# A two-block transformer kernel: loads, roundings and splits of its expert stages in another order, norm sums over two added tiles

## The reference, cut to what matters

```python
def rmsnorm(x, g):
    y = x * lax.rsqrt(jnp.mean(x * x, axis=-1, keepdims=True) + EPS)
    return y * g

def peer_ffn(h, w_q, sub_keys, u_tab, v_tab):      # h: normed, 512 x 1024
    q = (h @ w_q).reshape(B, L, 8, 2, 128)         # 8 heads, two halves
    s = einsum('blhpd,pnd->blhpn', q, sub_keys)    # 128 keys for each half
    top_s, top_i = lax.top_k(s, 16)
    ...                                            # the best 16 of the 16 x 16 sums, idx and gate
    act = gelu(einsum('bpd,bphkd->bphk', h, u_tab[idx]))
    return einsum('bphk,bphkd->bpd', act * gate, v_tab[idx])
```

## Time and profile before

| What | us |
|---|---|
| median of three runs | 2179.35 |
| the profiled execution | 2177.73 |
| its span | 2175.9 |
| TensorE busy (matmuls) | 2115.4 (97%) |
| VectorE busy | 1304.1 (60%) |
| GpSimd busy | 1033.5 (47%) |
| ScalarE busy | 922.6 (42%) |

### The profile page before, as it was taken

How to read it: one execution, slowest core, us unless ns; L and a number is a source line. 1 busy time by engine, 2 the same in 40 slices (tenths; PEclk the granted TensorE clock), 3 DMA queues, 4 the chain that set the end, 5 groups by cost and what they waited for, 6 DMA issues and landing times.

```text
span 2175.9 us, 27394 instructions
## 1 busy us (share of the span) xinstructions
PE 2115.4 (97%) x10296; PEld 1661.6 (76%) x10296; DVE 1304.1 (60%) x2244; ACT 922.6 (42%) x1528; POOL 1033.5 (47%) x892
## 2 busy tenths in 40 slices
PE   8999999999999999999999998999999899999999
PEld 6877767557887776887878877777778788888887
DVE  6456257352235774215898957888881666666664
ACT  4223343572234234111334447777773434343432
POOL 6655546212324122877859887999996100000000
PEclk9999999999999999999999999999999999999999
DMA  5222312201111111233216664777788988888884
GB/s 201 100 78 78 116 61 90 90 30 49 59 40 59 59 55 43 97 122 110 78 59 199 205 206 141 272 289 246 272 291 294 333 300 286 289 284 300 288 287 149
DMA packets 98291, 359.32 MB, mean 165 GB/s; under 512 B 8480, under 2 KB 41504, under 8 KB 73328
## 3 DMA queue, kind: packets, MB, share of 16 engines
q1 hardware_dynamic: 98160, 357.56, 47.3%
HBM read 286.09 MB, written 71.30 MB: 164 GB/s over the span
## 4 chain that ended last, share of the span: by engine, by line
PE 67%; POOL 13%; DVE 11%; issue 6%; ACT 2%; DMA 1%; POOLq 0%; SPq 0%; ACTq 0%; DVEq 0%
PE ps L1438 11%; PE ps L1439 11%; PE ps L802 10%; PE ps L803 9%; PE ps L804 9%; POOL area L2643 6%; POOL wring_parts L2621 6%; PE ps L791 2%; PE ps L1249 2%; DVE area L2413 2%; PE ps L1386 1%; PE ps L1387 1%; DVE area L2410 1%; PE ps L884 1%; PE ps L1225 1%
## 5 line engine op out<-in xcount | busy, mean ns | idle before, releaser
L2577 POOL CAST wring_parts<-wring 128x512 fp32r<-128x512 f32 x236 | 170.5, 764 | 546.0 <-PE ps L804 429.3
L1386 PE MATMUL ps<-sqbuf_parts,wring_parts 128*128 128x512 f32 x1024 | 412.6, 403 | 5.5 <-POOL wring_parts L2621 5.5
L1387 PE MATMUL ps<-normed_x_parts,wring_parts 128*128 128x512 f32 x1024 | 404.4, 395 | 0.0
L2621 POOL TENSOR_TENSOR wring_parts<-wring_parts,wring 128x512 fp32r<-128x512 f32 x256 | 331.0, 1323 | 76.0 <-ACT wring_parts L1856 73.0
L2581 POOL TENSOR_TENSOR wring_parts<-wring,wring_parts 128x512 fp32r<-128x512 f32 x244 | 351.2, 1470 | 6.6 <-ACT wring_parts L1852 1.5
L1386 PEld LDWEIGHTS ps<-sqbuf_parts,wring_parts 128*128 128x128 f32 x1024 | 194.0, 189 | 50.6 <-POOL wring_parts L2621 4.9
L1387 PEld LDWEIGHTS ps<-normed_x_parts,wring_parts 128*128 128x128 f32 x1024 | 193.9, 189 | 41.8
L802 PE MATMUL ps<-resid_parts,wring_parts 128*128 128x512 f32 (+1 forms) x528 | 201.2, 381 | 6.1 <-DVE normed_x_parts L2010 3.3
L803 PE MATMUL ps<-normed_x_parts,wring_parts 128*128 128x512 f32 (+1 forms) x528 | 197.0, 373 | 0.0
L804 PE MATMUL ps<-resid_parts,wring_parts 128*128 128x512 f32 (+1 forms) x528 | 196.2, 372 | 0.0
L1474 ACT ACTIVATE area<-ps 128x1024 f32<-128x1024 f32 (+6 forms) x89 | 61.7, 696 | 275.2 <-PE ps L804 183.5
(11 more groups left out here) (269 smaller groups left out, 4431.4 us busy)
## 6 DMA issues: line engine op xcount, KB each, us to landing
wring<-in_weights_dram SPq DMA_DIRECT2D x65, 1024.0 KB, 4.8
wring<-in_uT_dram SPq DMA_DIRECT2D x128, 512.0 KB, 4.4
area<-in_vT_dram SPq DMA_DIRECT2D x44, 1024.0 KB, 7.2
hidden_table<-area SPq DMA_DIRECT2D x32, 1024.0 KB, 6.7
gate_table<-area SPq DMA_DIRECT2D x32, 1024.0 KB, 8.4
area<-gate_table SPq DMA_DIRECT2D x32, 1024.0 KB, 9.1
wring<-in_vT_dram SPq DMA_DIRECT2D x20, 1024.0 KB, 6.7
rt<-hidden_table SPq DMA_DIRECT2D x32, 512.0 KB, 4.6
```

Source lines behind the costliest of these rows:

```text
L1386: pe.matmul(out, first[:, d], h_first[:, k, :], start=(k == 0), stop=False)
L1387: mm = pe.matmul(out, rest[:, d], h_rest[:, k, :], start=False, stop=(k == KD - 1))
L2577: ins = nc.gpsimd.tensor_copy(up[:, d, :], W(name)[:, d, :])
L2621: ins = nc.gpsimd.tensor_tensor(rest[:, a:a + PIECE], first[:, a:a + PIECE], u_raw[t % len(USLOT)][:, a:a + PIECE], ALU.subtract)
```

## The change

Five things are edited. The loads of the first two value halves are issued five tiles sooner, behind the wait for the stores of the stage's first half only. ScalarE rounds values 2 and 3 behind the first two coefficients, not among the last Gelus, and VectorE makes the rest of coefficients 1 ahead of that of values 2 and 3. ScalarE rounds tiles 0 and 1 at the start of its turn for head 6, and GpSimd splits them at the start of its turn for head 1, tiles 2 and 3 at the start of its turn for head 2. In the three norms VectorE adds the first three pairs into one tile (4), and TensorE sums tiles 4 and 6 alone. The copy of a quad into the stage runs over experts outside and tokens inside, where it ran the other way round; what is written is the same.

```diff
@@ -728,11 +730,12 @@
                 if t == EG * (BEFORE + BESIDE):
                     while parts:
                         store_piece(*parts.pop(0))
-                if t == TILES - len(USLOT) - 1:
+                if t == EG * (BEFORE + BESIDE) + 4:
 
                     sp.wait_ge(stored[0], 8 * PIECES * STORES)
                     load_v(0)
                     load_v(1)
+                if t == TILES - len(USLOT) - 1:
 
                     sp.wait_ge(stored[1], 8 * PIECES * STORES)
                     sp.wait_ge(spread, QUADS)
@@ -893,13 +896,15 @@
                 sq = norm_sq(name)[:, 0:KD * width].rearrange("p (k t) -> p k t", k=KD)
                 for m in pairs:
                     if name in ADDED:
-                        pe.wait_ge(pair_added, 4 * ADDED.index(name) + m + 1)
+                        if m >= 2:
+                            pe.wait_ge(pair_added, 2 * ADDED.index(name) + m - 1)
                     else:
                         pe.wait_ge(squares, 4 * BIG.index(name) + m + 1)
-                    for k in (2 * m,) if name in ADDED else (2 * m, 2 * m + 1):
+                    for k in ADDED_TILES[m] if name in ADDED else (2 * m, 2 * m + 1):
                         for at, n in ((0, T), (T, META)) if width == TM else ((0, T),):
                             mm = pe.matmul(flat(key)[:, at:at + n], ones, sq[:, k, at:at + n],
-                                           start=(k == 0), stop=(m == 3 and k == (6 if name in ADDED else 7)))
+                                           start=(k == ADDED_TILES[2][0] if name in ADDED else k == 0),
+                                           stop=(k == ADDED_TILES[3][0] if name in ADDED else k == KD - 1))
                 if pairs[-1] == 3:
                     fills(mm, key)
 
@@ -1857,12 +1862,12 @@
                                ).then_inc(u_rounded, 1)
 
             for h in range(HP):
+                if h == HP - 2:
+                    round_u(0)
+                    round_u(1)
                 if h + 1 < HP:
                     query(h + 1)
                 copy_out(("ps", h), sc[:, h].rearrange("p a b -> p (a b)"), flat(("ps", h)))
-                if h == HP - 2:
-                    round_u(0)
-                    round_u(1)
             round_u(2)
             round_u(3)
 
@@ -1927,12 +1932,13 @@
                 for j in range(EG):
                     gelu(g, j)
                     beside(EG * g + j)
-                    if g >= GROUPS - 2 and j % 2:
-                        if (g, j) == (GROUPS - 2, 1):
-                            act.wait_ge(stored[1], 8 * PIECES * STORES)
-                        round_v(2 * (g + 2 - GROUPS) + j // 2)
+                    if g == GROUPS - 2 and j % 2:
+                        round_v(j // 2)
             for n in range(2):
                 round_coefs(n)
+            act.wait_ge(stored[1], 8 * PIECES * STORES)
+            round_v(2)
+            round_v(3)
             round_coefs(2)
             round_coefs(3)
             for n in range(CSLOTS, HALVES):
@@ -1999,7 +2005,14 @@
 
                 sq = sqbuf[:, 0:KD * width].rearrange("p (k t) -> p k t", k=KD)
                 dve.wait_ge(squares, 4 * BIG.index(name) + m + 1)
-                dve.tensor_tensor(sq[:, 2 * m, :], sq[:, 2 * m, :], sq[:, 2 * m + 1, :], ALU.add).then_inc(pair_added, 1)
+                ins = dve.tensor_tensor(sq[:, 2 * m, :], sq[:, 2 * m, :], sq[:, 2 * m + 1, :], ALU.add)
+                if m in (1, 2):
+                    link(ins)
+                    ins = dve.tensor_tensor(sq[:, 2 * m, :], sq[:, 2 * m, :], sq[:, 2 * m - 2, :], ALU.add)
+                if m < 2:
+                    link(ins)
+                    return
+                ins.then_inc(pair_added, 1)
 
             def split_norm(turn, name, gain, width, between={}):
 
@@ -2499,9 +2512,9 @@
                 if i == 0 and piece >= 2:
 
                     dve.wait_ge(stored[piece % 2], 16 * STORES * (piece // 2))
-                dst = stage[:, piece % 2, :].rearrange("p (j t) -> p t j", t=HALF)
+                dst = stage[:, piece % 2, :].rearrange("p (j t) -> p j t", t=HALF)
                 dve.wait_ge(spread, n + 1)
-                dve.tensor_copy(dst[:, 4 * i:4 * i + 4, :], spread_out(n)).then_inc(copied, 1)
+                dve.tensor_copy(dst[:, :, 4 * i:4 * i + 4], spread_out(n).rearrange("p t n -> p n t")).then_inc(copied, 1)
 
             def split_v(n):
                 dve.wait_ge(v_rounded, n + 1)
@@ -2541,9 +2554,9 @@
             multiply_coefs(0)
             multiply_coefs(1)
             split_coefs(0)
+            split_coefs(1)
             split_v(2)
             split_v(3)
-            split_coefs(1)
             for n in range(2, HALVES):
                 multiply_coefs(n)
                 if n >= CSLOTS:
@@ -2624,8 +2637,8 @@
 
             split = 0
             for h in range(HP):
-                if h == 2:
-                    for split in range(4):
+                if h in (1, 2):
+                    for split in range(2 * h - 2, 2 * h):
                         split_u(split)
                 weigh_places(h)
                 if h < 2:
```

More of the change, by code:

```diff
@@ L302 @@
 ADDED = ["post", "mix", "ffn"]
+ADDED_TILES = ((), (), (4,), (6,))
 def build(nc, A):
```

## The result

The changed kernel takes 2186.06 us (median of 12 runs, 2183.57 to 2190.26) against 2178.05 us for the kernel before (12 runs, 2172.72 to 2183.91): a ratio of 1.004, 95% interval 1.0031 to 1.0049. It is 8.0 us slower; the forecast was 8.8 slower. The profiled execution took 2190.26 us, the slowest of the twelve, with a span of 2188.5, 12.6 above the span of the one before.

A forecast was written before the change was run, and what follows sets the result against it. TensorE, two thirds of the chain of waits, was taken as the bound. Terms 15.9 + 1.6 - 1.8 - 1.4 - 1.4 - 1.8 - 1.7 - 0.5 + 0.9 - 1 = +8.8 on the 2179.35 us median gave 2188, range 2173 to 2200.

The forecast's parts named there:

- The first tiles' split: GpSimd waits for tile 0 ahead of the last query's weights; less waiting and no low clock at tile 0: together +14.3 us.
- the three terms ahead of tile 0: Last query starts later, +15.9 us; low clock after that idleness, +1.6; shorter TensorE wait before tile 0, -1.8.
- The "-1.4": At tile 0, TensorE's shorter idleness of about 1.1 us brings no low clock: -1.4 us.
- Both sides move by the same amount, and that slack stays: End of routing: VectorE runs some 14.5 us later, its 11.9 us wait for turned entries stays; no cost.
- Handover: Second expert stage: no ScalarE wait for the first value tile, -1.4 us; a value rounding moved behind the coefficients, -1.8.
- Norms: Fewer sum matmuls on TensorE: post -1.7 us, ffn -0.5, mix +0.9 from a longer idle stretch with low clock.
- Copy: VectorE's copy into the stage lies between 701 and 1089 ns, shortening only the spreading stage's start: -1 us.
- (b): Strided PSUM read exceeds VectorE's spare time; above 1.5 us a copy, each further 0.1 costs 13 us; chance 0.12.
- (a): GpSimd before the last query: tile 0 is rounded early, no hold-up; sum -8.7 us, 2170.6; chance 0.08.
- (c): Spreading stage: a faster copy returns TensorE's idleness there and at its start, down to 2173 us; chance 0.09.
- (d): Tile loads behind the value loads leave TensorE without a tile: +4 us, 2192; chance 0.04.

## Why the prediction was right

The sign, the cause and the size held. Step by step, with the second pair of profiles beside the first (its spans differ by +8.9 us, those of the first by +12.6):

- **The first tiles' split, +14.3.** The gap ahead of the last query grew by 15.84 us (forecast 15.9), by the order of work that the step gives: the tile's rounding, two tiles, places, weights. All of it lies 2.7 us earlier than written (the copy ahead of the rounding at 1115.82 for 1118.55, the first split at 1117.86 for 1120.6, the last query at 1132.71 for 1135.5). Half of that is chance: when the kernel before was profiled again, it was 1.4 us earlier at the same place. Counted from the last sum of the ffn norm, tile 0 starts behind 104.06 us in both profiles of before and behind 119.79 and 119.86 in those of after: +15.7 and +15.8, where the three terms ahead of tile 0 (15.9 + 1.6 - 1.8) give 15.7. After the gap the last query's first matmul took 0.77 us (0.47 before), the low clock of the step; and tile 0 waited 1.31 us in place of 2.94, at the full clock. The "-1.4" held too: tile 1 starts 3.79 us behind tile 0 in both profiles of after, 5.23 and 5.35 in those of before. In the second profile of before the first four matmuls of tile 0 still ran at the full clock (0.47 us for the first), and the clock fell behind them, as its window shows:

```profile
1135.70:1138.70 3.00, 2.77 (x9) 2.24 (x10) 2.97 (x19) 2.54 (x3) 3.00 (x4) 0.72 0.00 0
```

- **"Both sides move by the same amount, and that slack stays": no term.** The slack did stay: VectorE waits 12.0 us for the turned entries, 11.9 before. What the step had no term for is TensorE's waits for later splits, which VectorE's long additions bring about: 4.9 us in the profile of after, 1.4 in that of before. By the terms the stretch behind tile 0 was to shrink by 1.4 us (the low clock). It grew by 3.6 in the first pair, and shrank by 1.5 in the profiles taken again (176.0 against 177.5), where the waits are 2.9 and 3.2 us. So the missing term is one of chance: it is nothing in one pair of profiles and 5 us in the other, and the medians (+8.0) don't ask for it.
- **Handover, -3.2.** Alone -3.9, and -3.7 by the stretch of the trace. The wait of 7.11 us went and TensorE's short gaps with it, the idleness before the combine fell from 4.74 to 2.94 (forecast -1.8). The late expert tile, 6.20 us, cost nothing, as taken: TensorE has no wait between the spreading stage and the combine.
- **Norms, -1.3.** Post gave 1.72 us (forecast 1.7) and ffn 0.4 (forecast 0.5). Mix was mis-sized: the low clock behind its longer wait takes back 1.4 to 1.6 us in four profiles and about 2.7 in two, where the step took 0.9. By the traces the three give 0.5 to 0.7 us, or cost about 0.6. The medians can't tell -1.1 from nothing.
- **Copy, -1.** The duration fell to the ordered copy's (690 ns beside the 701 of the earlier trace rows), and no run shows that it was worth anything. The term came from the idle start of the spreading stage, which was 5.5 us idle after and 4.8 before: VectorE's copy doesn't set it. Rival (b) fell with the same row, since the read of PSUM at a step of 512 bytes has no price. The Trainium skill, "SBUF — State Buffer" (the note under "Door 1: The DMA port swizzle"), has lines of 16 bytes for SBUF and 8 for PSUM. It asks for at least two accesses in a line of SBUF for the full rate, and the trace agrees: two neighbours of 4 bytes run at that rate (414 ns for 256 elements), single elements don't (1089 ns for 512, 690 in runs of four). For reads of PSUM, where each element falls into another line, no run shows a penalty (the same 690 ns).

The rivals: (a) fell with the 16.93 us; (c) with the copy alone; (d), expert tiles late by the value loads, came as a wait of ScalarE and stopped there.

By their ratios the parts measured alone are worth 0.76 - 0.16 - 0.09 - 0.02 = 0.49%, 10.7 us, and the whole is 0.40%, 8.7 us. The intervals of the four reach 0.1 to 0.2% to each side, so the 2 us between the two are no interaction that these runs could show.

That the forecast came within 0.8 us of the median is partly luck. With the old order put back, the order is worth +11.2 and the rest -3.2, where the terms have +14.3 and -5.5; alone the order cost 16.1. The two misses cancel. The traces support the +14.3 to a few tenths, so the medians' 11.2 and 16.1 say more about the scatter of runs than about that term.

## What to carry to other kernels

Before putting work earlier on an in-order engine, look up when its input is ready: an item that waits takes its place in front of everything behind it, and a gap in a timeline is only free behind the items that can already run. Here the same two splits cost 16 us ahead of the weights and gave 5 back behind them.

One profile is one draw. Where two engines contend for something, take a second profile of the unchanged program before you explain a difference of a few microseconds between two traces.

## What the hardware showed

- VectorE's additions with both inputs in SBUF waited while GpSimd's subtraction ran: 0.69 us the pair alone, 2.7 to 2.9 beside splits of 1.25 us each, and now and then 6.5 to 14.3 us, until GpSimd paused between tiles or had two splits of its batch left. The Trainium skill, "SBUF — State Buffer" ("SBUF: two separate sides"), calls the pair of ports between these two engines an exclusive lock, held for a whole instruction. The usual 2.7 us agrees with that (one instruction waited for by each addition). The long ones go further than the page: in the longest, VectorE's addition came to its turn only behind eleven instructions of the batch. Which it will be is decided by something finer than the trace: in head 2's batch, pairs that started 1.32 to 1.37 us behind its start took 2.9 us in nine profiles, and 10.4, 10.4 and 14.3 us in three whose starts (1.35, 1.37 and 1.34) lie among those of the nine. What decides it stays open.
- GpSimd's side shows it too: a run of twelve splits takes 15.31 to 15.42 us when VectorE got in between, 15.04 to 15.08 when it didn't. That is a quick way to find such a pair in a timeline.
- TensorE's granted clock fell behind a wait of 2.94 us in seven of eight profiles (tile 1 5.2 to 5.4 us behind tile 0 in place of 3.79), behind one of 3.49 us in six of six, and behind one of 1.31 us in none of six. It can fall a few matmuls late: behind the same 2.94 us tile 0's first matmul took 0.76 us in one execution and 0.47 in another, and both lost 1.4 to 1.6 us. So the first matmul's duration doesn't tell whether a gap costs the clock; the granted clock of the next few microseconds does.
